# Seven block products for the up projection of both feed-forward stages, with x kept in DRAM meanwhile

## What is computed

```python
def rms_norm(x, g):
    y = xf * lax.rsqrt(jnp.mean(xf * xf, axis=-1, keepdims=True) + EPS)
    return (y * g)
def sq_relu_ffn(h, w1, w2):                 # w1: 1024 x 4096, w2: 4096 x 1024
    return jnp.square(jax.nn.relu(h @ w1)) @ w2
# per layer
x = x + mixer(rms_norm(x, norm_mix_g))      # ends with concat(att, gated) @ w_out
x = x + sq_relu_ffn(rms_norm(x, norm_ffn_g), w_ffn1, w_ffn2)
```

## Time and profile before

| | us |
|---|---|
| runs, median of 3 | 2534.32 |
| profiled execution, its own time | 2534.72 |
| its span, first to last instruction | 2533.0 |
| TensorE busy (matmuls) in the span | 2451.2 |
| DVE, POOL, ACT busy | 1484.3, 1407.5, 776.7 |
| up projection of layer 0 on TensorE | 552.8 to 927.4 |
| down projection of layer 0 on TensorE | 927.4 to 1269.7 |
| up projection of layer 1 on TensorE | 1803.4 to 2178.1 |
| down projection of layer 1 on TensorE | 2178.1 to 2514.5 |

### The profile page before, as it was taken

The page is one execution under the profiler, slowest core; times in us unless marked ns, Lnnn a source line. Parts: engine busy times, 40 slices in busy tenths (PEclk is TensorE's granted clock), DMA queues, the critical chain, the costliest instruction groups (busy, mean ns, idle before and its releaser), DMA issues.

```text
span 2533.0 us, 42346 instructions
## 1 busy us (share of the span) xinstructions
PE 2451.2 (97%) x17227; PEld 2317.3 (91%) x17227; DVE 1484.3 (59%) x1988; ACT 776.7 (31%) x1164; POOL 1407.5 (56%) x1035
## 2 busy tenths in 40 slices
PE   8999999999999999999989999989999999999998
PEld 7998866999999999999978998669999999999998
DVE  4324389444343358777868879764434333687777
ACT  4200178321010133334238832652101010433331
POOL 4433256255455458887952334963455544788784
PEclk9999999999999999999999999999999999999999
DMA  6111120212443354444240111002143344544441
GB/s 225 34 50 35 43 94 2 86 50 103 152 146 120 139 192 158 152 133 155 63 148 18 51 34 55 19 18 102 34 153 139 118 148 169 188 133 147 160 127 78
DMA packets 128201, 264.10 MB, mean 104 GB/s; under 512 B 15517, under 2 KB 81141, under 8 KB 123478
## 3 DMA queue, kind: packets, MB, share of 16 engines
q1 hardware_dynamic: 125446, 245.17, 28.4%
q10 hardware_dynamic: 2640, 17.31, 1.8%
HBM read 173.72 MB, written 87.93 MB: 103 GB/s over the span
## 4 chain that ended last, share of the span: by engine, by line
PE 66%; POOL 16%; issue 9%; DVE 7%; ACT 2%; DMA 0%; POOLq 0%; SPq 0%; DVEq 0%; ACTq 0%
PE PS L284 51%; POOL w L2161 8%; PE PS L328 4%; PE PS L1109 1%; PE PS L1170 1%; POOL stage L2151 1%; POOL stage L2155 1%; POOL stage L2153 1%; PE PS L1520 1%; POOL stage L2157 1%; PE PS L1147 1%; PE PS L1549 1%; PE PS L1489 1%; DVE Bq L473 1%; POOL Lb L1884 1%
## 5 line engine op out<-in xcount | busy, mean ns | idle before, releaser
L284 PE MATMUL PS<-h,w_sp 128*128 128x352 f32 (+1 forms) x5184 | 859.8, 325 | 19.4 <-DVE h L738 6.6
L284 PEld LDWEIGHTS PS<-h,w_sp 128*128 128x128 f32 (+1 forms) x5184 | 841.5, 189 | 26.8 <-issue 21.2
L2119 POOL TENSOR_TENSOR w_sp<-stage,ones 128x512 fp32r<-128x512 f32 x244 | 266.0, 1122 | 836.8 <-PE PS L284 790.8
L328 PE MATMUL PS<-Bq,w 128*128 128x264 f32 x5280 | 649.4, 285 | 15.3 <-DVE aux L481 8.8
L328 PEld LDWEIGHTS PS<-Bq,w 128*128 128x128 f32 x5280 | 646.3, 189 | 18.3 <-DVE aux L481 9.3
L284 PE MATMUL PS<-hz,w_sp 128*128 128x352 f32 x3456 | 567.0, 323 | 0.0
L284 PEld LDWEIGHTS PS<-hz,w_sp 128*128 128x128 f32 x3456 | 557.7, 188 | 0.0
L2161 POOL TENSOR_TENSOR w<-stage,w 128x512 fp32r<-128x512 f32 x220 | 338.2, 1561 | 141.6 <-ACT w L378 141.6
L2127 POOL TENSOR_TENSOR w_sp<-stage,w_sp 128x512 fp32r<-128x512 f32 x244 | 370.2, 1548 | 0.0
L446 DVE SCALAR_TENSOR_TENSOR ob<-PS,rstd 128x1056 f32<-128x1056 f32 x64 | 80.5, 1257 | 398.0 <-PE PS L284 397.9
L368 ACT ACTIVATE ob<-ob 128x1056 f32<-128x1056 f32 x64 | 69.6, 1088 | 609.8 <-DVE ob L446 609.8
(11 more groups left out here) (309 smaller groups left out, 2234.4 us busy)
## 6 DMA issues: line engine op xcount, KB each, us to landing
hid_spill<-ob SPq DMA_DIRECT2D x32, 2112.0 KB, 7.6
stage<-in_w_ffn SPq DMA_DIRECT2D x64, 1024.0 KB, 7.7
Bq<-hid_spill SPq DMA_DIRECT2D x112, 528.0 KB, 3.7
stage<-in_w_in_even SPq DMA_DIRECT2D x10, 1024.0 KB, 4.9
stage<-in_w_in_odd SPq DMA_DIRECT2D x9, 1024.0 KB, 5.1
x_spill<-xT ACTq DMA_DIRECT2D x2, 4224.0 KB, 13.6
xT<-x_spill ACTq DMA_DIRECT2D x2, 4224.0 KB, 12.8
xtok<-in_x_prompt SPq DMA_DIRECT2D x8, 512.0 KB, 8.6
```

The source lines that it names most:

```text
L284: mm = pe.matmul(out[0:m, c, :], lhs, rhs(k, b)[:, c * CH:(c + 1) * CH], start=(i == 0 and n == 0), stop=(i == nk - 1 and n == 2))
L328: mm = pe.matmul(out[:, c, :], w2_of(c0, q, i)[:, a, m * P:(m + 1) * P], Bq[q][:, b, i, c * QN:(c + 1) * QN], start=(i == 0 and n == 0), s ...
L2119: pool.tensor_tensor(w_sp[:, s, 0, q:q + 512], stage[:, s, q:q + 512], ones[:, 0:1].to_broadcast([P, 512]), ALU.mult).then_inc(w_hi_done, 1)
```

## The change

The up projection gets the same form as the down projection. A pair of tiles (256 hidden rows) by the 1024 rows of x by 1056 columns is a 2 by 2 by 2 block product: hidden halves of 128, halves of k (blocks 0 to 3 and 4 to 7), column halves of 528. It becomes seven products, each of 4 blocks k, 3 pairs of parts and 2 column chunks of 264, so 24 matmuls, in the order `UP_ORDER`. Four of them accumulate on top of an earlier product in the same PSUM banks; ACT copies the partial results out (`copy`) before they are overwritten, and DVE adds them (`add`).

- POOL no longer makes the high parts of the up weights; ACT does (`up_high`). POOL makes four combinations and seven low parts per pair (`up_split`), DVE seven combinations and conversions of x per block, ACT their high parts.
- The combinations of x (`up_lo`, `up_hi`, `xT` itself) use the space of `xT`, `h` and `hz`, so ACT stores each block of x to DRAM as it becomes final, scales it in place after the store has landed, and SP loads all of x back near the end of the up projection (`x_rows`).
- The output projection takes its tiles in the order 0, 4, 1, 5, 2, 6, 3, 7 (`M_ORDER`), its weights loaded as two pieces of 128 columns.
- POOL changes `xT` (`xa_fix`) and makes the last pair's combinations (`last_combine`) between the weights of the first down chunk.

```diff
+UP_ORDER = [0, 3, 4, 1, 5, 6, 2]
+M_ORDER = [0, 4, 1, 5, 2, 6, 3, 7]
+LATE = [1, 6, 5, 2]
...
+        def up_product(pe, L, n, q, d=0):
+
+            N, pos = 16 * L + n, UP_ORDER.index(q)
+            pe.wait_ge(wl_done, 112 * L + 7 * N + pos + 1 + d * 7)
...
+            if q == 4:
+                pe.wait_ge(uc_done, 3 * N + 1 + d * 3)
+            if q == 1 and n:
+                pe.wait_ge(ue_done, 4 * (N - 1) + 4 + d * 4)
+            if q == 5:
+                pe.wait_ge(uc_done, 3 * N + 3 + d * 3)
+            if q == 2:
+                pe.wait_ge(ue_done, 4 * N + 2 + d * 4)
+            out = up_pair(L, n, {1: 1, 3: 2, 6: 2}.get(q, 0))
+            fresh = q in (0, 1, 3)
+            for k in range(4):
+                if n == 0:
+                    ul_ready(pe, L, q, k)
+                for i, (a, b) in enumerate(((0, 0), (0, 1), (1, 0))):
+                    for c in range(2):
+                        mm = pe.matmul(out[:, c, :], w_up[L][q][:, a, k * P:(k + 1) * P],
+                                       up_rhs(q, k, b)[:, c * QN:(c + 1) * QN], start=(fresh and k == i == 0),
+                                       stop=(k == 3 and i == 2), skip_group_check=not fresh)
+            mm.then_inc(ut_done, 1)
...
+            def unit(n, d=0, nxt=True):
+
+                if n:
+                    square(n - 1, 1, d)
+                copy(n, 1, d)
+                up_high(act, L, n + 1, 0, d)
+                copy(n, 2, d)
+                up_high(act, L, n + 1, 3, d)
+                copy(n, 3, d)
+                up_high(act, L, n + 1, 4, d)
+                up_high(act, L, n + 1, 1, d)
+                up_high(act, L, n + 1, 5, d)
+                square(n, 0, d)
+                up_high(act, L, n + 1, 6, d)
+                up_high(act, L, n + 1, 2, d)
...
+            copy(0, 1)
+            for k in range(4):
+                late(1, k)
+            copy(0, 2)
+            for k in range(4):
+                late(6, k)
+            late(5, 0)
+            root(0)
+            root(1)
+            copy(0, 3)
+            for k in range(1, 4):
+                late(5, k)
+            root(2)
+            for k in range(4):
+                late(2, k)
...
+                dve.tensor_tensor(halves(ob_at(n, b)), up_pair(L, n, role), halves(x), ALU.add).then_inc(ue_done, 1)
+                dve.wait_ge(ue_done, 4 * N + e + d * 4)
+                r = rstd[:, (b % 2) * HN:(b % 2) * HN + HN]
+                dve.scalar_tensor_tensor(ob_at(n, b), ob_at(n, b), 0.0, r, ALU.max, ALU.mult).then_inc(ur_done, 1)
...
+            for i, k in enumerate(M_ORDER):
+                evacuated(act, jo + i)
+                if i >= 2:
+                    act.wait_ge(ss_add, 7 * L + i - 1)
+                act.activation(rstd[:, :] if i == 0 else sqt[:, :], xT[:, k, :], ACT.Square).then_inc(sq_done, 1)
+                act.dma_start(spill_k[:, k, :], xT[:, k, :]).then_inc(u_spill, 16)
+                g = (G_FFN, G_FFN + 8)[L] + k
+                dst = xg7[:, :] if k == 7 else xT[:, k, :]
+                if k < 7:
+                    act.wait_ge(u_spill, 16 * (8 * L + i + 1))
+                act.activation(dst, xT[:, k, :], ACT.Copy, scale=gv[:, g:g + 1]).then_inc(ug_done, 1)
...
+                if i == 5:
+                    for q in (0, 3, 4, 1):
+                        up_high(act, L, 0, q)
+                if i == 6:
+                    for q in (5, 6, 2):
+                        up_high(act, L, 0, q)
...
+                for pos, q in enumerate(UP_ORDER):
+                    if q == 3:
+                        pool.wait_ge(v_stage[n % 2], 16 * (16 * L + n // 2 + 1) + d * 8)
+                        pool.tensor_tensor(a21, a21, a22, ALU.add).then_inc(s_rdy, 1)
...
+                    pool.wait_ge(wh_done, 112 * L + 7 * N + pos + 1 + d * 7)
+                    lo, hi = (w_up[L][q][:, x, :].rearrange("p (k n) -> p k n", k=4) for x in (1, 0))
+                    pool.tensor_tensor(lo, up_block((n + FS[L]) % 2, q), hi.bitcast(F32),
+                                       ALU.subtract).then_inc(wl_done, 1)
...
+                down_weights(1)
+                store(14)
+                sp_.wait_ge(ut_done, 7 * (16 * L + 15) + 2)
                 hidden(0, 0)
...
+                x_rows(4)
+                hidden(0, 3)
+                hidden(0, 4)
                 store(15)
+                sp_.wait_ge(hid_st[1], 16 * (8 * L + 8))
+                hidden(0, 5)
+                hidden(0, 6)
```

More of the change, by code:

```diff
@@ L391, in prepare @@
                         b_high(c - 1, 6, d)
-                    if q == 6 and first:
-                        act.wait_ge(hid_st[1], 16 * (8 * L + 8))
                     w_high(c, q, d)
@@ L484, in down @@
                 ins.then_inc(pt_free, 1)
-            up(0, stored=L > 0)
-            up(1, stored=L > 0)
-            with dve.Fori(0, 6) as i:
-                up(2, i * 2)
-                up(3, i * 2)
-            up(14)
+            for q in (1, 6):
+                for k in range(4):
+                    late(q, k)
+            late(5, 0)
+            raw_t4(dve, L, 3)
+            for k in range(1, 4):
+                late(5, k)
+            dve.wait_ge(rt_done, 3 * L + 3)
+            ch.link(dve.reciprocal(rstd[:, :], rstd[:, :]))
+            dve.wait_ge(u_spill, 16 * 8 * (L + 1))
+            add(0, 1)
+            for k in range(4):
+                late(2, k)
+            add(0, 2)
+            add(0, 3)
+            straight(0)
+            for n in (1, 2, 3):
+                up(n)
+            with dve.Fori(0, 2) as i:
+                for n in (4, 5, 6, 7):
+                    up(n, i * 4)
+            for n in (12, 13, 14):
+                up(n)
+            combine(14)
+            add(15, 1)
+            add(15, 2)
             b_low(0)
+            add(15, 3)
+            straight(15)
             b_low(1)
-            dve.wait_ge(hid_st[1], 16 * (8 * L + 7))
-            evacuate(15, 0)
-            evacuate(15, 1)
-            dve.wait_ge(xa_fix, 4 * L + 4)
             for q in range(7):
+                if q == 1:
+                    dve.wait_ge(xr_back, 32 * L + 16)
+                if q == 2:
+                    dve.wait_ge(xa_fix, 4 * L + 4)
                 for m in range(4):
-                    if q == 0 and m == 2:
-                        combine(15)
                     down(4 * q + m, q, m, first=True)
-                for n in ((2,), (3,), (4,), (5, 6), (7, 8), (9, 10), (11,))[q]:
+                for n in ((2,), (3,), (4,), (5,), (6, 7), (8, 9), (10, 11))[q]:
                     b_low(n)
@@ L553, in x_tile_ready @@
                 eng.wait_ge(xT_ready, NTT)
[L554 removed]
+            else:
                 L = n // 2 - 1
@@ L2114, in split_high @@
                 s = wslot(u)
-                pool.wait_ge(w_stage[s], 16 * (u // 2 + 1) + ds)
+                pool.wait_ge(w_stage[s], 16 * sum(1 + (v in OUT_UNITS) for v in range(s, u + 1, 2)) + ds)
                 if u >= 2:
@@ L2148, in split_down @@
                         for i in range(2):
-                            a11, a21, a12, a22 = (stage[:, i, 512 * x:512 * x + 512] for x in range(4))
+                            a11, a21, a12, a22 = (stage[:, (i + FS[L]) % 2, 512 * x:512 * x + 512] for x in range(4))
                             if q == 3:
@@ L2206, in _ @@
             pool_odd(pool)
-            for u in range(U_OOUT + 1, U_F1):
+            for u in range(U_OOUT + 1, U_OOUT + 4):
                 split(u)
-            split_ffn(1, U_F1, 5)
+            split_up(1)
             down_all(1)
```

511 lines of the change are left out of this document (335 added, 176 removed).

## The result

The changed kernel takes 2506.3 us (median of 4 runs, 2503.3 to 2509.0), the kernel before beside it 2535.3 us (4 runs, 2533.2 to 2536.4): ratio 0.9886, 95% interval 0.9869 to 0.9904. That is 28.9 us less, inside the range and 6 us above the forecast of 2500. The profiled execution took 2503.25 us, its span is 2501.5 against 2533.0 before. Cut at the first and last matmuls of each stage, the two profiled spans differ as follows; the last column is the prediction's term.

What follows compares the result with a forecast made beforehand. TensorE was taken to bound both stages. Up projection -18.5 us per layer (start +21.3, pairs -39.8), -37.0 for two, plus 2.7 into the down projection, gave -34.3 us from 2534.3: 2500 us, range 2470 to 2530.

Steps and rivals of the forecast that it cites:

- The steady pairs: Up projection, pairs 1 to 15: 20.5 us per pair in place of 23.15, -39.8 us per layer.
- Its own need: Up projection, steady pairs: POOL's work, waits for ACT and loss to DVE take 17.0 to 20.9 us per pair.
- the forecast's sign: Sign that the forecast is right: POOL busy over 80% in the steady up stage.
- the 0.8: Steady up pairs: POOL loses 0.8 of each two-SBUF-operand DVE instruction's length, 3.9 us per pair.
- the rival in which POOL sets the pace: Up projection: POOL and DVE exclude each other fully, a pair takes 21.9 us, total 2542 us; chance 0.15.
- The start: Start of each up projection: pair 0 waits for a chain and takes 48.9 us, 21.3 more than before.
- six blocks put the seventh at 549: Output projection: from DVE's first addition at 478.12, blocks at a mean of 11.8 us bring the seventh at 549.
- the forecast's chain: Pair 0: ones-matmuls from 571, reciprocal from 584 to 590.7, product 7 at 595.6, pair ended at 601.7.
- The rival of a cheap start: Start of up projection: stores land in about 2 us, pair 0 takes 36 us, total 2474 us; chance 0.18.
- That is 13.7 a layer: Down projection loss: 1.5 us before product 5, 6.7 at hidden blocks, 3.2 for the clock, 2.28 at the end.
- The 1.5 us put down for product 5 of pair 15: Last up pair: ACT stands for late down weights before copies 2 and 3, so product 5 waits some 1.5 us.
- The rival of a slower transition: Stores or transition slower: 8 to 12 us more at each start or transition, total 2516 to 2526; chance 0.12.

Runs made afterwards that it cites:

- the lead raised in steps: Against the changed kernel: last pair's combinations and xT differences on VectorE, its low parts three products ahead, four from mid chunk 3, five from mid chunk 5; 2485.3 us.

## Why the prediction held, and where its steps failed

**The steady pairs: right.** 20.5 us per pair was forecast, 20.29 measured: shorter matmuls lose nothing, and TensorE waits for nobody. Over 15 pairs that is some 3 us a layer better than forecast.

**POOL: right in the pace, wrong in who pays.** Its own need was put at 17.0 to 20.9 us; it is 18.1, and POOL is busy 153.00 of 202.22 us, 76%, where the forecast's sign said over 80%. For the forecast let POOL lose 3.9 us per pair to VectorE. Groups of both engines from 700 to 860 us of the changed kernel (some eight pairs):

```profile
L2431 POOL TENSOR_TENSOR w_up<-stage,w_up 128x512 fp32r<-128x512 f32 x56 | 79.4, 1430 | 39.4 <-ACT w_up L443 39.4
L2422 POOL TENSOR_TENSOR stage<-stage 128x512 f32<-128x512 f32 x7 | 12.3, 1755 | 0.0
...
L628 DVE SCALAR_TENSOR_TENSOR ob<-ob,rstd 128x528 f32<-128x528 f32 x24 | 31.1, 1295 | 0.8
...
L645 DVE TENSOR_TENSOR ob<-ob 128x528 f32<-128x528 f32 x8 | 14.3, 1793 | 0.0
```

VectorE's instructions with two SBUF operands, 0.70 us alone, take 1.30 to 1.79 us, but for one combination at 0.83; POOL's low parts go from 1.28 to 1.43, one of its four sums to 1.76, the other three stay at 1.29. POOL loses some 1.5 us per pair. VectorE pays most of the collision, and here it has the room (125 of 202 us busy); in the down stage it had not, as the 5.77 us row above shows. The row from which the 0.8 was taken showed it already: beside POOL's 2.0 us lost, two instructions of VectorE took 4.64 us in place of 2.5, and the sum held only POOL's part. So the rival in which POOL sets the pace didn't come, though the two engines do get in each other's way. The Trainium skill (SBUF — State Buffer, section "SBUF: two separate sides") says that whichever of the two starts first keeps the port pair for its whole instruction; the long VectorE instructions here agree with that in part. A rule of one instruction at a time would let VectorE in after one of POOL's, 1.3 us, but VectorE's 5.77 us lasted through four of them and its 11.69 us through more; the measurement decides.

**The start: mechanism right, size too dear by 11 us a layer.** The step that failed is "six blocks put the seventh at 549", at 11.8 us a block. The additions of blocks one and seven in the timeline of VectorE, with the reciprocal and the late low parts behind them:

```profile
478.18 1.26 DVE L831 TENSOR_TENSOR xT<-PS,xT 128x1056 f32<-128x1056 f32 x1 [12.53 <-DMA xT<-x_spill]
542.07 1.24 DVE L831 TENSOR_TENSOR xT<-PS,xT 128x1056 f32<-128x1056 f32 x1
...
571.77 6.74 DVE L681 RECIPROCAL rstd<-rstd 128x1056 f32<-128x1056 f32 x1
580.19 5.75 DVE L613 TENSOR_TENSOR up_hi<-xT,up_hi 128x528 fp32r<-128x528 f32 x4
```

A block took (542.07 - 478.18) / 6 = 10.65 us. The store, put at 3.7 us, takes 2.6, which is nearly the whole difference of 1.15; below TensorE's 11.57 the late first addition is caught up (the sixth, at 530.24, already waits 0.73 us for TensorE). That makes 7 of the 11 us. The other 4 are pair 0's four weight blocks, which were to hold ACT until 554: in ACT's timeline they end at 545.74. So product 1 follows the eighth tile at 553.29 as if nothing had been added, where the forecast had that tile leave PSUM at 564.7. From there the forecast's chain holds, 11 us earlier: the ones-matmuls at 560.3 in place of 571, the reciprocal at 571.8 in place of 584, 7.63 us before product 7 where "some 6" stood (the four low parts took 5.75 us, not 2.8, beside POOL). The slower clock behind that gap cost 591.03 - 586.66 = 4.37 less 20.29 / 7 = 2.90, 1.5 us, not 3.2. The rival of a cheap start named just this, faster stores, and its 36 us for pair 0 is nearer to 37.7 than the forecast's 48.9.

**Into the down projection: the step that failed is "That is 13.7 a layer".** For the sixth product of layer 0 it was right: combinations forecast 44 us after the start of pair 15 (at 875.2), so at 919, and ended at 919.81; the parts forecast at 932.8, and ready at 933.96; a loss of 6.7 + 3.2 = 9.9 us forecast, 8.51 of gap and 1.5 of clock measured. The end of the stage keeps its gap, 2.27 us. The 1.5 us put down for product 5 of pair 15 didn't come: its last four products take 11.93 us, against 11.75. In layer 1 the sixth product waited 0.32 us, and the 4.21 before the fourth came from VectorE's long wait beside POOL, for which the forecast had no term. And the sum ended with the sixth product's gap. The same backlog on POOL makes the second chunk's weights late: behind the sixth product come 0.84 + 4.55 + 3.76 us of gaps and 8.19 - 6.06 = 2.1 us of clock, 11.3 us in layer 0 which no term held, of a whole loss of 355.0 - 327.0 = 28.0; layer 1 lost 352.4 - 327.0 = 25.4. The runs show the cause in the second chunk: its gaps shrink when POOL's two insertions go to VectorE, and leave it when VectorE's lead is shortened, though then they come back later.

**The range** held the time since the two sizes err in opposite directions. Its sum was near by luck; its signs, but for the down stage of layer 0 (-1.6 forecast, +12.7 measured), were right, and in layer 0 its places too, but for the second chunk. The rival of a slower transition put 8 to 12 us more on each transition, and that came, 14 and 12; its total didn't, since the start gave as much back.

What stays open is part of the remaining 16 to 22 us a layer above 224 tiles of 1.46 us with the lead raised in steps: of 37.5 us in both layers TensorE idled 27.1 behind VectorE's additions, and no run here takes the rest apart. Nor does any run move POOL's instructions so that VectorE gets in between them.

## What to carry to other kernels

When strict queues hand work round in a ring, a delay isn't paid once at the first product that feels it: follow the late engine's backlog until it has spare time, and look at what the next stage's loads wait for. Then lighten the engine that is behind and win a lost lead back in small steps; a changed order that took no work off the late engine only moved the gap, in six runs of this study. Where two engines hold each other up, look for single instructions that take several times their usual time: they mark a dense list on the other engine. And take an unknown transfer's cost from both bounds through the whole chain: 1.1 us less per store turned a chain that falls behind TensorE into one that catches up.

## What the runs showed of the hardware

Where VectorE and GpSimd both read two SBUF operands, VectorE lost far more in the up stage (0.70 us grew to means of 0.83 to 1.79) than GpSimd (1.28 to means of 1.29 to 1.76), while in the earlier trace rows both lost alike, 2.1 us over two instructions and 2.0 over four. Beside GpSimd instructions that followed each other without a pause, single VectorE instructions of 0.70 and 1.25 us took 6.34, 5.77 and 11.69 us and ended 0.6 to 1.1 us after GpSimd paused. A store of 528 KB from SBUF to DRAM landed after 2.6 us. GpSimd's subtraction with an operand of four runs of 128 elements takes 1.28 to 1.30 us when nothing collides, as the contiguous one does.
